# Eleven of the 32 dot products of the modulation rows placed earlier, and their row given a place of its own

## The reference, cut to what matters

```python
m = jax.nn.silu(cond) @ p['w_ada'] + p['b_ada']            # 6 * 1024 numbers
sh1, sc1, g1, sh2, sc2, g2 = [m_lat[:, i:i + 1] for i in range(N_MOD)]
h = modulate(x, p['norm1_g'], sh1, sc1)
x_next = x + g1 * token_mixer(h, p, attend_latent)
x_next = x_next + g2 * peer(modulate(x_next, p['norm2_g'], sh2, sc2), p)
```

## Time and profile before

| | |
|---|---|
| median of the runs (lowest, highest) | 2184.88 us (2182.25, 2191.21) |
| span of the profiled execution, first to last instruction | 2185.6 us |
| mean granted clock of PE | 0.968 |
| busy: PE, DVE, ACT, POOL | 90%, 63%, 48%, 48% |
| DMA | 534.27 MB, mean 244 GB/s |

### The profile page before, as it was taken

One profiled execution on the slowest core, in us unless ns is written; L12 is line 12 of the kernel. 1 busy time (PEld: TensorE's weight loads), 2 busy tenths in 40 slices (PEclk: granted clock), 3 DMA queues, 4 the chain that ended last, 5 costly groups with the idle time before them and its releaser, 6 DMA issues.

```text
span 2185.6 us, 26292 instructions
## 1 busy us (share of the span) xinstructions
PE 1959.7 (90%) x9022; PEld 1434.6 (66%) x9022; DVE 1387.7 (63%) x2870; ACT 1041.4 (48%) x1957; POOL 1045.3 (48%) x844
## 2 busy tenths in 40 slices
PE   6999988897778777877999999999999999999998
PEld 2867767732333333333699777888879977778887
DVE  5758864676666676665377643278854775326887
ACT  3523545322122122121546687466664568846665
POOL 0733576664444444443687567700038865782000
PEclk9999999999999999999999999999999999999999
DMA  8523874899999999999555454545545545454553
GB/s 298 186 87 118 264 248 155 312 421 421 422 421 421 421 421 421 422 421 409 192 178 164 131 175 147 183 145 191 194 155 177 179 126 170 149 183 153 195 193 106
DMA packets 111445, 534.27 MB, mean 244 GB/s; under 512 B 12496, under 2 KB 12880, under 8 KB 77904
## 3 DMA queue, kind: packets, MB, share of 16 engines
q1 hardware_dynamic: 67536, 245.30, 34.0%
q0 software_dynamic: 38720, 275.96, 30.8%
q10 hardware_dynamic: 5056, 11.34, 1.6%
HBM read 531.43 MB, written 1.11 MB: 244 GB/s over the span
## 4 chain that ended last, share of the span: by engine, by line
PE 60%; DMA 22%; ACT 6%; DVE 5%; issue 4%; POOL 2%; ACTq 0%; SPq 0%; DVEq 0%; POOLq 0%
PE psum L885 58%; DMA pair_rows<-in_peer_uv,arena 9%; DMA arena<-in_peer_uv,arena 8%; DMA wring<-in_peer_uv,arena 4%; PE psum L964 2%; ACT w_hi L1496 1%; POOL w_lo L2932 1%; ACT arena L1507 1%; POOL w_lo L2930 1%; DVE arena L2878 1%; DMA wring<-in_w_ada 1%; ACT arena L1870 1%; DVE w_lo L1979 0%; ACT arena L1741 0%; ACT arena L1888 0%
## 5 line engine op out<-in xcount | busy, mean ns | idle before, releaser
L885 PE MATMUL psum<-w_hi,a_parts 128*128 128x512 f32 (+1 forms) x2112 | 673.0, 394 | 22.0 <-POOL w_lo L2932 11.8
L2930 POOL TENSOR_TENSOR w_lo<-wring,w_hi 128x512 fp32r<-128x512 f32 x282 | 377.8, 1340 | 522.6 <-ACT w_hi L1496 511.7
L1496 ACT ACTIVATE w_hi<-wring 128x1024 fp32r<-128x1024 f32 (+1 forms) x414 | 431.3, 1053 | 282.8 <-PE psum L885 247.5
L885 PE MATMUL psum<-a_parts,w_hi 128*128 128x256 f32 (+1 forms) x1952 | 483.3, 329 | 9.0 <-DVE a_parts L2574 7.5
L885 PEld LDWEIGHTS psum<-w_hi,a_parts 128*128 128x128 f32 x2112 | 396.6, 189 | 118.1 <-POOL w_lo L2932 14.7
L885 PE MATMUL psum<-arena 128*128 128x512 f32 (+7 forms) x1148 | 338.8, 457 | 84.4 <-ACT arena L1741 50.8
L885 PE MATMUL psum<-w_lo,a_parts 128*128 128x512 f32 (+1 forms) x1056 | 409.4, 388 | 0.0
L2932 POOL TENSOR_TENSOR w_lo<-wring,w_hi 128x512 fp32r<-128x512 f32 x282 | 394.7, 1400 | 0.0
L885 PE MATMUL psum<-a_parts,w_lo 128*128 128x256 f32 (+1 forms) x1344 | 376.9, 280 | 0.0
L885 PEld LDWEIGHTS psum<-a_parts,w_hi 128*128 128x128 f32 x1952 | 331.1, 192 | 42.0 <-issue 7.9
L885 PEld LDWEIGHTS psum<-arena 128*128 128x128 f32 (+2 forms) x1148 | 185.5, 199 | 217.4 <-issue 120.2
(11 more groups left out here) (266 smaller groups left out, 2105.8 us busy)
## 6 DMA issues: line engine op xcount, KB each, us to landing
wring<-in_w_up SPq DMA_DIRECT2D x88, 512.0 KB, 4.0
wring<-in_w_xbc SPq DMA_DIRECT2D x48, 512.0 KB, 4.2
wring<-in_w_dn SPq DMA_DIRECT2D x44, 512.0 KB, 3.8
wring<-in_w_adaT SPq DMA_DIRECT2D x32, 512.0 KB, 4.4
wring<-in_w_qkv SPq DMA_DIRECT2D x32, 512.0 KB, 3.6
wring<-in_w_z SPq DMA_DIRECT2D x32, 512.0 KB, 3.8
wring<-in_w_g SPq DMA_DIRECT2D x32, 512.0 KB, 3.9
wring<-in_w_ps SPq DMA_DIRECT2D x32, 512.0 KB, 3.7
```

Of the source, the lines that this page charges most:

```text
L885: mm = lambda o, a, b, start, stop: nc.tensor.matmul(o, a, b, start=start, stop=stop, skip_group_check=True)
L1496: a.reaches(A(w_hi[:, n % SPLIT_RING, 0:width], wring[:, c % RING, 0:width], ACT.Copy), hi_ready, n + 1)
L2930: nc.gpsimd.tensor_tensor(w_lo[:, r, 0:half], wring[:, c % RING, 0:half], w_hi[:, r, 0:half].bitcast(F32), ALU.subtract)
```

## The change: what it does

- The eight late dots (`LATE_AFTER`, `LATE_AT`) and the three behind the last head's scores are gone from their places. Dots 0 to 3 now stand on DVE behind the twelve `zhy`, 4 to 6 behind `zqkv` 0 and 1, and 7 to 10 behind the first convolution (behind `y1`); the other 21 stay at three per head for heads 2 to 8.
- Their chunks stand at matching places in the order of the weights: four between the second and the third chunk of `zqkv` 0 and 1, three behind its fourth, four ahead of the last group of four.
- The row keeps the whole of `dve_junk` from the start of the hyena part; the temporaries `tmp_a` and `tmp_y` move to the arena, which grows by 64 numbers per partition.
- POOL fetches the row at the start of its stream, after `ada` 3 and the filters; ACT applies Silu behind the ninth `zhy`.
- On ACT, the conversions up to the second chunk of `w_hy_out` stand ahead of the sigmoids of gates 0 to 5.
- All 32 sums get their bias in one addition; the second one, behind the first selection of `peer`, is gone, and with it the second value of the semaphore `ada_cols`.

```diff
-ADA_FIRST, ADA_DOTS, DOTS_PER_HEAD, LATE_DOTS = 4, 32, 3, 8
-LATE_AFTER = [("nao", NA_HEADS - 1)] * 4 + [("mix", 3)] * 2 + [("mT", 3)] * 2
-LATE_AT = [4, 4, 5, 6, 9, 10, 12, 12]
+ADA_FIRST, ADA_DOTS, DOTS_PER_HEAD = 4, 32, 3
+DOTS_BEFORE = ADA_DOTS - DOTS_PER_HEAD * (NA_HEADS - 1)
+DOTS_AFTER = {("zhy", 11): range(0, 4), ("zqkv", 1): range(4, 7), ("spec", 7): range(7, DOTS_BEFORE)}
...
+    at = len(w)
     rows("w_in", "zqkv", 3, lambda j: ((0, 1), (2, 5), (6, 9))[j])
+    for place, after in ((at + 8, ("spec", 7)), (at + 4, ("zqkv", 1)), (at + 2, ("zhy", 11))):
+        w[place:place] = [("w_adaT", None, n, CHUNK, turn[after] + 1, True, False) for n in DOTS_AFTER[after]]
     for h in range(1, NA_HEADS + 1):
...
-        w.extend(("w_adaT", None, DOTS_PER_HEAD * (h - 1) + i, CHUNK, turn[("nao", h - 1)] + 1, True, False)
-                 for i in range(DOTS_PER_HEAD))
-    at = len(w)
+        if h < NA_HEADS:
+            w.extend(("w_adaT", None, DOTS_BEFORE + DOTS_PER_HEAD * (h - 1) + i, CHUNK, turn[("nao", h - 1)] + 1, True,
+                      False) for i in range(DOTS_PER_HEAD))
...
-    for n in reversed(range(LATE_DOTS)):
-        w.insert(at + LATE_AT[n], ("w_adaT", None, ADA_DOTS - LATE_DOTS + n, CHUNK, turn[LATE_AFTER[n]] + 1, True, False))
...
-    tmp_a = dve_junk[:, 0:512]
+    tmp_a = area(A_M + 3072, 512)
+    tmp_y = area(A_M + 3584, SEQ)
+    c_row = dve_junk[:]
...
+            if m_ == 8:
+                act.wait_ge(S("c_row_in"), 16)
+                a.reaches(A(c_row, c_row, ACT.Silu), S("c_row_ready"), 1)
...
-            if h == 0:
-                act.wait_ge(S("c_row_in"), 16)
-                a.reaches(A(dve_junk[:], dve_junk[:], ACT.Silu), S("c_row_ready"), 1)
             if h == NA_HEADS:
+                weights_upto(act, "w_hy_out", None, 1)
                 gates_out(range(6))
...
+        ada_dots(DOTS_AFTER[("zhy", 11)])
         dve.wait_ge(S("bias_qkv_in"), 16)
...
         for n in range(2):
             projected(n)
+        ada_dots(DOTS_AFTER[("zqkv", 1)])
...
+            if o_ == 0:
+                ada_dots(DOTS_AFTER[("spec", 7)])
...
-        early = ADA_DOTS - LATE_DOTS
-        ada_dots(early - DOTS_PER_HEAD, early)
         gate_bias(NA_HEADS // 2 - 1)
         na_low(NA_HEADS - 1)
         v.settle()
-        tt(ada_col[:, 0:early], ada_sum[:, 0:early], V("b_ada", 16, early), ALU.add)
+        tt(ada_col, ada_sum, V("b_ada", 16, ADA_DOTS), ALU.add)
...
-        late_dot("nao", NA_HEADS - 1)
...
-            late_dot("mix", n)
...
-            late_dot("mT", k)
...
-        late = slice(ADA_DOTS - LATE_DOTS, ADA_DOTS)
-        v.settle()
-        v.reaches(T.tensor_tensor(ada_col[:, late], ada_sum[:, late], V("b_ada", 40, LATE_DOTS), ALU.add),
-                  S("ada_cols"), 2)
...
+        pool.wait_ge(psum_filled, turn[("ada", 3)] + 1)
+        pool.wait_ge(S("filters_ready"), 2)
+        pool.dma_start(c_row, row_b("c_row", 0, D)).then_inc(S("c_row_in"), 16)
         wait_filled(pool, "hcT", KD - 1)
...
-                pool.dma_start(dve_junk[:], row_b("c_row", 0, D)).then_inc(S("c_row_in"), 16)
```

More of the change, by code:

```diff
@@ L468, in build @@
     small = sb("small_values", 1024)
-    ARENA = 24520
+    ARENA = 24584
     arena = sb("arena", ARENA)
@@ L1186, in _, with gate_rows @@
         branch_columns("w_hy_out", 0, 1)
-        def gate_rows(name, first, part):
-            pe.wait_ge(S("ada_cols"), part)
+        def gate_rows(name, first):
+            pe.wait_ge(S("ada_cols"), 1)
             for n in range(2):
@@ L1208, in _ @@
         merged_turned("mT", merged, 0, 1)
-        gate_rows("gb", 0, 1)
+        gate_rows("gb", 0)
         columns_of_rows("w_out", None, [("wout", 0), ("wout", 1)], [0, 0], early=True,
@@ L1264, in first_columns @@
             close(m)
-        gate_rows("gb2", 24, 2)
+        gate_rows("gb2", 24)
         for t in range(TT):
@@ L2204, in _, with ada_dots @@
         v.settle()
+        ada_chunks = [c for c, w in enumerate(wplan) if w[0] == "w_adaT"]
+        def ada_dots(ns):
+            dve.wait_ge(S("c_row_ready"), 1)
+            for n in ns:
+                c = ada_chunks[n]
+                w = wring[:, c % RING, :]
+                dve.wait_ge(weights_in[c % RING], 16 * (c // RING + 1))
+                v.reaches(T.tensor_tensor_reduce(out=w, in0=w, in1=c_row, scale=1.0, scalar=0.0, op0=ALU.mult,
+                                                op1=ALU.add, accum_out=ada_sum[:, n:n + 1]), S("ada_dots"), n + 1)
+        ada_dots(DOTS_AFTER[("zhy", 11)])
         dve.wait_ge(S("bias_qkv_in"), 16)
@@ L2230, in roped_rows @@
             for t in range(TT):
-                row, t2 = qkv[:, t, 512 * part:512 * part + 512], dve_junk[:, 0:512]
+                row, t2 = qkv[:, t, 512 * part:512 * part + 512], tmp_a
                 tt(heads(na_sq[:, t, :]), heads(row), rope_gc[:, t, part:part + 1, :].to_broadcast([P, 8, HD]), ALU.mult)
@@ L2309, in _ @@
                 projected(n)
-            src, tmp_y = (zcT, y1T)[o_], dve_junk[:, 512:512 + SEQ]
+            src = (zcT, y1T)[o_]
             for m_ in range(HY_T):
@@ L2340, in gate_bias @@
                                                  ALU.add))
[L2342 to L2356, removed]
         masked_bias(0)
@@ L2376, in _ @@
             if h:
-                ada_dots(DOTS_PER_HEAD * (h - 1), DOTS_PER_HEAD * h)
+                ada_dots(range(DOTS_BEFORE + DOTS_PER_HEAD * (h - 1), DOTS_BEFORE + DOTS_PER_HEAD * h))
             if h:
```

## The result

The changed kernel is slower: 2193.14 us (median of 19 runs, 2187.03 to 2198.16) against 2183.89 us (19 runs, 2176.44 to 2191.21) for the one before. The medians differ by 9.25 us; the ratio on record is 1.0039, with an interval of 1.0030 to 1.0047 (8.5 us). The prediction said 2179.0, and its range ended at 2186.5. The profiled span grew from 2185.6 to 2191.8 us, by 6.2.

A forecast was written before the change was run, and what follows sets the result against it. PE was taken as nearly full in the hyena part, with waits for `w_adaT` transfers, dots and low parts behind the attention. -11.1 - 4.0 - 0.2 + 9.4 = -5.9 us gave a median of 2179; 8 in 10 between 2169.5 and 2186.5.

The forecast's parts named there:

- Dots 7 to 10: Hyena part, around `spec`: these dots fit DVE's 5.71 us of free time and cost nothing.
- The start of the attention: Silu and its table loads leave the chain: 4.0 us less (2.57 wait, 1.59 restart); PE's own queue is late next.
- Dots 4 to 6 and the restart: Before `spec`: conversion waiting for dot 4's ring place delays `vrow`, 5.7 us lost; PE's slow restart 1.5 more.
- Dots 0 to 3 and Silu: `zqkv` 0 and 1: POOL's last low part is ready late for PE, 2.2 us lost (bounds 0 and 3.8).
- the hyena part: Sum of the losses where the moved dots go: 9.4 us more, bounds 5.4 and 14.1.
- Behind the attention: From `mix` 0 to `w_out`: eleven dots leave, 11.1 us less, bounds 4.3 and 12.2.
- (a): Behind the attention: DVE no longer waits for `w_adaT` and merges `mix` 4 and 5 during PE's 5.56 us of products.
- (b): Behind the attention: without dots a chunk's low parts cost POOL 2.6 against PE's 2.78; `w_hy_out`'s fourth chunk is converted earlier.
- the conversion put ahead: ACT converts `w_hy_out`'s first chunk before copying `nap` 12 and 13: 1.06 us on the path to `nao` 6.
- the costless `vrow`: Rival, chance 0.25: the wait before `vrow` costs next to nothing, only the 2.2 loss stays, 2171.8 us.
- the low parts as the bound behind the attention: Rival, chance 0.15: POOL's low parts still set the pace there, saving only 4.3, 2185.8 us.
- The late landings: Rival, chance 0.1: transfers in the hyena part land after 6.5 us twice, loss 14.1, 2183.7 us.

The follow-up runs named there:

- x5: Kernel before, no dot moved, POOL's low parts of the last two chunks of `zqkv` 6 to 9 put behind its wait for `spec` 7: 2191.55 us.
- x1: Changed kernel with the chunks of dots 7 to 10 loaded behind all of `zqkv`, dots staying in place: 2180.93 us, 0.9979 of before.
- x7: Kernel before with only the row's own place, its early transfer and the early Silu, all dots unmoved: 2182.05 us, 0.9980 of before.
- x2: Changed kernel with ACT's copies of `vrow` ahead of the four waiting conversions for `zqkv` 2 to 5: 2182.3 us, 0.9983 of before.
- x4: Kernel before without the eleven dots that the change moves, their sums set to zero: 2174.2 us, 0.9952 of before.
- x6: Changed kernel with POOL's low parts of the last two chunks of `zqkv` 6 to 9 ahead of its wait for `spec` 7: 2187.91 us.
- x3: Changed kernel with dots 7 to 10's chunks behind all of `zqkv` and `vrow` copies ahead of the waiting conversions: 2174.09 us, 0.9947 of before.
- x8: The kernel of x3 with head 7's copies of `nap` ahead of the first conversion of `w_hy_out`: 2170.7 us, 0.9931 of before.

## Why the prediction was wrong

*The step that failed*, in its own words: "Dots 7 to 10 fit DVE's 5.71 us while POOL has no low part to make, and the products that they would delay are needed only after 7.12 us of `spec` and four chunks: nothing". The dots do fit. What the step left out is the ring: for dots 4 to 6 I asked which chunk takes the place of a dot and where its conversion then stands; for dots 7 and 8 I didn't. So POOL has low parts to make just there: six halves in one run, one DVE instruction held for 7.34 us, and +5.9 in the stage; x5 makes the same 5.9 in this stage without a dot, x1 takes it away.

*The start of the attention*: "What is late next is PE's own queue". It was DVE, by the same cause, and with PE's clock at its lower level. The term of 4.0 (2.57 + 1.59 make 4.16) is confirmed in size (x1 3.8, x7 3.7) and was lost whole, +1.0 instead of -4.0. These two, 5.9 + 5.0 = 10.9 us, are most of the 12.1 between the -5.9 forecast and the +6.2 of the spans. None of the rivals had this mechanism; the range ended 6.6 us too low, and the time lies above even the 2192.1 to which the prediction's worst bounds add up.

*Dots 4 to 6 and the restart*: the chain was right, the terms too small, and the prediction looked at dot 4's chunk alone, where the three chunks ahead of it hold ACT nearly as long. 5.7 was 6.7, and 1.5 for the restart was 2.6 (x2): the transfer took 4.35, not 3.7, and behind the rest of 7.52 us the granted clock is 0.55 from 126 to 132 us; the 1.5 came from a rest of 2.57. *Dots 0 to 3 and Silu*: 2.2 was 1.3 (the stage of x2 against before); PE's wait for POOL there is 1.38. For these terms the bounds hold: with both, the hyena part lost 10.7, not 9.4. With the 5.9 of the second stall it lost 16.6, above its upper bound of 14.1 (which the terms given, 3.8, 8.5 and 1.5, make 13.8).

*Behind the attention*: the mechanism was right; 11.1 was 12.8 in the kernel after, a little above the bound of 12.2, and 11.0 in x4, both against the profile of before; against x5 and x7 the two are 10.6 and 8.9. Conditions (a) and (b) both came true; the conversion put ahead cost 0.95 (forecast 1.06).

*The rivals*: the costless `vrow` is refuted by the hole of 7.52; the low parts as the bound behind the attention by 22.20 us of products without a wait. The late landings were true in part (4.35 in the kernel after, 6.30 and 7.64 in x1 and x6).

## What to carry to other kernels

When a piece of work is moved into a ring of buffers, follow each place that it holds to the next user of that place, on every engine that orders its work by when places come free: the work itself may fit and still push another engine's step past a wait. A helper engine's work that is done early in idle time is worth something even when nobody waits for it yet, because done late and all at once it can collide with the engine that is then on the path. The order of four chunks alone decided here between 9.25 us slower and 3.6 us faster than before (after and x1); with the order of ACT's conversions put right as well, it was 10.4 to 14.9 us faster (x3 and x8).

## What the runs showed of the hardware that was not expected

- A DVE instruction with two operands in SBUF waited for a whole run of POOL instructions, not for the one in progress: 7.34, 7.36 and 7.30 us (after, x2, x5) beside six halves of 1.3 without a gap, where it takes 0.69 alone. It doesn't always: in x6, where the halves come in pairs, DVE's operation of 1.61 starts during the first half (177.13 to 178.42) and ends at 178.96, while the second half, which follows at once, takes 1.74 instead of 1.3. There DVE waited for one half only. The kernel after shows the same from 187.46 us on, beside the next pair. DVE's dots, which also read two operands in SBUF, took turns even with a run of four halves: 2.20 to 2.30 each (after, 106.8 to 115.7 us). The Trainium skill, SBUF — State Buffer, section SBUF: two separate sides, says that a DVE operation with two inputs in SBUF and a GpSimd operation that reads SBUF contend for one shared pair of ports, and that whichever starts first has it for its whole instruction. That DVE stands still agrees; by that rule it would have waited for one half, some 1.3 us, as it does beside the pairs, and beside the run of six the traces show five more. What sets the run of six apart wasn't tried.
- Behind three waits of 1.33, 1.08 and 1.08 us between short transposes the granted clock fell from 1.00 to the lower level, which then held through full work up to 220 us: 5.62 instead of 2.94 us for 16 scores. x2, x5 and x6 show the same behind such waits; x1, without them, keeps 1.00. Shorter rests can go either way: behind the same waits of 1.10 and 0.79 us, the transform `spec` 4 to 7 took 8.8 us in x3, x4 and x5 and 7.1 in the other seven traces.
